# Last FFN output of a two-layer encoder on one core: sixteen of its 43 row blocks, instead of fourteen, by seven block products a pair

## The reference

```python
h = rmsnorm(x, norm_ffn[l])
gu = h @ w_ffn_in[l]
g = causal_dwconv(gu[..., :D_FF], ffn_conv_w[l], ffn_conv_b[l])
x = x + (jax.nn.silu(g) * gu[..., D_FF:]) @ w_ffn_out[l]
...
return rmsnorm(x, final_norm)
```

## Time and profile before

| What | us |
|---|---|
| median of three runs | 2070.26 |
| lowest, highest | 2069.8, 2071.41 |
| the profiled execution, its own time | 2071.34 |
| its span, first to last instruction | 2069.5 |
| PE busy | 2055.3 (99%) |
| DVE busy | 1492.8 (72%) |
| ACT busy | 1104.3 (53%) |
| last FFN output, first to last matmul | 1829.0 to 2059.1 |

### The profile page before, as it was taken

How to read it: one execution, slowest core, us unless ns; L and a number is a source line. 1 busy time by engine, 2 the same in 40 slices (tenths; PEclk the granted TensorE clock), 3 DMA queues, 4 the chain that set the end, 5 groups by cost and what they waited for, 6 DMA issues and landing times.

```text
span 2069.5 us, 32420 instructions
## 1 busy us (share of the span) xinstructions
PE 2055.3 (99%) x11522; PEld 1785.3 (86%) x11522; DVE 1492.8 (72%) x2115; ACT 1104.3 (53%) x1539; POOL 23.5 (1%) x20
## 2 busy tenths in 40 slices
PE   9999999999999999999999999999999999999998
PEld 8888888888888888888888888888888888888886
DVE  7998777676666676554489978667666767679887
ACT  6556655555555554443364656455555555555554
POOL 0001100000000000000000011000000000000000
PEclk9999999999999999999999999999999999999999
DMA  8554455655555655555565544555555565545564
GB/s 291 176 183 162 138 188 178 205 189 191 192 182 187 199 192 192 194 187 193 199 215 193 178 159 136 192 190 193 194 189 187 182 202 186 192 161 201 199 225 158
DMA packets 108370, 390.58 MB, mean 189 GB/s; under 512 B 12161, under 2 KB 12673, under 8 KB 107905
## 3 DMA queue, kind: packets, MB, share of 16 engines
q1 hardware_dynamic: 106416, 384.35, 55.6%
q10 hardware_dynamic: 1872, 5.13, 0.8%
HBM read 387.33 MB, written 2.10 MB: 188 GB/s over the span
## 4 chain that ended last, share of the span: by engine, by line
PE 97%; DVE 2%; DMA 0%; ACT 0%; issue 0%; ACTq 0%; DVEq 0%
PE bank L1414 54%; PE bank L1417 27%; PE bank L1670 3%; PE bank L1671 3%; PE bank L1672 3%; PE bank L1501 2%; PE bank L1490 1%; PE bank L1492 1%; PE bank L1491 1%; DVE wlo L1118 1%; PE bank L1554 0%; DMA par<-params 0%; PE bank L1666 0%; PE bank L1577 0%; ACT whi L675 0%
## 5 line engine op out<-in xcount | busy, mean ns | idle before, releaser
L1414 PE MATMUL bank<-xg,whi 128*128 128x512 f32 x3648 | 1136.6, 393 | 2.2 <-DVE wlo L858 2.2
L878 DVE TENSOR_TENSOR wlo<-raw,whi 128x1024 fp32r<-128x1024 f32 x642 | 780.5, 1222 | 490.1 <-ACT whi L498 489.4
L498 ACT ACTIVATE whi<-raw 128x1024 fp32r<-128x1024 f32 x642 | 673.7, 1057 | 577.2 <-PE bank L1417 559.3
L1417 PEld LDWEIGHTS bank<-xg,wlo 128*128 128x128 f32 x3648 | 685.7, 188 | 151.4
L1417 PE MATMUL bank<-xg,wlo 128*128 128x256 f32 x3648 | 720.5, 279 | 0.0
L1414 PEld LDWEIGHTS bank<-xg,whi 128*128 128x128 f32 x3648 | 553.5, 188 | 6.3 <-issue 3.3
L1414 PE MATMUL bank<-hidden,whi 128*128 128x512 f32 x688 | 213.4, 392 | 0.0
L1414 PE MATMUL bank<-mix,whi 128*128 128x512 f32 x512 | 160.7, 395 | 0.0
L1417 PEld LDWEIGHTS bank<-hidden,wlo 128*128 128x128 f32 x688 | 129.2, 188 | 28.3
L1417 PE MATMUL bank<-hidden,wlo 128*128 128x256 f32 x688 | 135.7, 279 | 0.0
L503 ACT ACTIVATE half<-bank 128x256 f32<-128x256 f32 x228 | 86.1, 382 | 63.7 <-PE bank L1417 61.2
(11 more groups left out here) (191 smaller groups left out, 1449.3 us busy)
## 6 DMA issues: line engine op xcount, KB each, us to landing
raw<-wstream SPq DMA_DIRECT2D x725, 512.0 KB, 3.3
pw_sb<-pww ACTq DMA_DIRECT2D x2, 1024.0 KB, 6.7
outT<-xt SPq DMA_DIRECT2D x8, 256.0 KB, 2.9
x<-xT SPq DMA_DIRECT2D x2, 512.0 KB, 9.8
gains<-gain_rows ACTq DMA_DIRECT2D x1, 1024.0 KB, 6.0
raw<-wstream SPq DMA_DIRECT2D x2, 256.0 KB, 4.5
x<-xT ACTq DMA_DIRECT2D x2, 256.0 KB, 5.5
x<-xT SPq DMA_DIRECT2D x2, 256.0 KB, 7.0
```

Source lines behind the costliest of these rows:

```text
L498: nc.scalar.activation(whi[:, s, slot_cols(rel)], raw[:, s, :], ACT.Copy).then_inc(hi_ready, 1)
L878: nc.vector.tensor_tensor(wlo[:, s, slot_cols(rel)], raw[:, s, :], whi[:, s, slot_cols(rel)], ALU.subtract).then_inc(lo_ready, 1)
L1414: nc.tensor.matmul(ps[bank][:], whi[:, s, blk * P:blk * P + P], mov, start=first, stop=False)
L1417: return nc.tensor.matmul(ps[bank][:, 0:S], wlo[:, s, blk * P:blk * P + P], mov[:, 0:S], start=False, stop=last)
```

## The change

There are eight pairs, (3, 4), (8, 9) and so on to (38, 39), in place of seven that began with (8, 9). So 27 ordinary pieces are left for each half, not 29. They no longer stand by three between pairs but by two or three, by a table for each half. Two of the four batches of factors move: behind slots 25 and 38 instead of 26 and 40; the fourth batch is now of two pairs. All else is unchanged, and every line behind the table is two lines further down.

```diff
-PAIRED = [(8 + 5 * i, 9 + 5 * i) for i in range(7)]
+PAIRED = [(3 + 5 * i, 4 + 5 * i) for i in range(8)]
 SINGLE = [k for k in range(FC) if not any(k in pair for pair in PAIRED)]
 LEAD = (8, 4)
+BETWEEN = ((2, 2, 3, 2, 2, 3, 2, 3), (3, 3, 3, 2, 3, 2, 3, 2))
...
     lead, rest = SINGLE[:LEAD[u]], SINGLE[LEAD[u]:]
     units = [(k,) for k in lead]
-    for i, pair in enumerate(PAIRED):
-        units += [pair] + [(k,) for k in rest[3 * i:3 * i + 3]]
-    return units + [(k,) for k in rest[3 * len(PAIRED):]]
+    for pair, n in zip(PAIRED, BETWEEN[u]):
+        units += [pair] + [(k,) for k in rest[:n]]
+        rest = rest[n:]
+    return units + [(k,) for k in rest]
...
-COMBS_AT = (5, 12, 26, 40)
+COMBS_AT = (5, 12, 25, 38)
```

## The result

The changed kernel takes 2077.59 us (median of seven executions, 2075.25 to 2078.12) against 2070.32 us for the kernel before: a ratio of 1.0033, 95% interval 1.0022 to 1.0043. That is 7.3 us slower; the forecast was 5.0 us slower, 2075.2 us, with a range of 2072.0 to 2077.6 us. The profiled execution took 2075.25 us with a span of 2073.0 us and is the shortest of the seven. Of all executions timed for this text one, of 5323 us in experiment 10, lies far outside the others; without it that experiment's median would be 2071.45 us instead of 2071.51.

What follows compares the result with a forecast made beforehand. PE, busy 99% of the span, was taken to bound the kernel, able to wait only for DVE. Terms -1.36 + 1.58 + 0.25 + 2.7 + 1.8 gave +5.0 us on 2070.26: 2075.2 us, range 2072.0 to 2077.6.

Steps and rivals of the forecast that it cites:

- the four stalls: PE idle before fe of slots 15, 28, 40 and before the last piece: about 1.8, 1.0, 2.5 and 1.7 us.
- The clock falls: Rival: half clock once or twice behind a 2.5 us stall, 1.7 us each; 2077 to 2079 us; 8%.
- Part 1: Added pair, once in each half: seven products in place of eight, six matmuls fewer, 1.36 us less on PE.
- Part 2: Gaps of two without extra work: DVE ready 1.1 us before PE is due; cost nothing, or 0.1 us.
- Part 3: Second batch, slot 12: PE arrives 2.72 us earlier at fe, DVE only 1.14; stall grows by 1.58 us.
- Part 4: Third batch, slot 25, gap of three, now behind the second piece: net +0.25 us of stall.
- Part 5: Fourth batch, slot 38, gap of two, now two pairs: PE waits for DVE before fe, +2.7 us.
- Part 6: End of second half: upper corrections delay the last piece's low half, so PE stalls, +1.8 us.
- The sum of 5.0: Whole kernel: saved products and added stalls together make it 5.0 us slower, median 2075.2 us.
- The estimate for a DVE step of 1.22 us: DVE's step between low halves: 1.22 instead of 1.14 us would add some 0.3 and 0.4 us to Part 3 and Part 4.
- The signs: Trace checks: 984 matmuls; wrong if PE waits at more places than the four stalls and the change of halves.
- The parts named for "same": Whole kernel, no measurable change: rest of forecast, fourth batch or end costing little, DVE keeping up; 0.31.

Runs made afterwards that it cites:

- experiment 10: Kernel before, seven pairs, with one ordinary piece moved from the second batch's gap to the end of the first half: 2071.51 us, ratio 1.0005.
- experiment 1: The changed kernel again, unaltered, against the kernel before: 2076.88 us against 2070.21, ratio 1.0031.
- experiment 11: As 9, with the last two single batches behind slots 30 and 42 and four pieces behind the first half's last pair: 2068.09 us, ratio 0.9989.
- experiment 8: Kernel before, seven pairs in old order, factors in smaller batches (two pairs behind slots 5 and 7, one behind 12, 26, 40): 2068.74 us, ratio 0.9992.
- 9: Against experiment 7: single batches behind d slots 11, 18, 25, 31, and three pieces instead of two behind the first half's last pair: 2067.95 us, ratio 0.9987.
- experiments 6: Changed kernel, eight pairs, pieces reordered: gaps of three where factor batches are made, seven pieces behind the second half's last pair: 2074.85 us, ratio 1.0020.
- experiment 4: Kernel before, seven pairs, three ordinary pieces moved from the second half's end to its front, four hooks three slots later: 2072.51 us, ratio 1.0011.
- Experiment 2: Changed kernel, upper corrections of the second half behind the low half of the very last piece instead of ahead of it: 2076.98 us, ratio 1.0033.
- Experiment 3: Changed kernel, fourth batch of factors behind slot 43, in a gap of three, instead of slot 38: 2074.0 us, ratio 1.0017.
- Experiment 5: Kernel before, with five extra DVE operations, results unused, behind the sums of the second half's last pair: 2075.98 us, ratio 1.0027.
- experiment 7: Piece order of experiment 6, with smaller batches of factors: two pairs behind slots 5 and 7, one behind 11, 13, 25, 38: 2071.99 us, ratio 1.0005.

## Why the prediction was right, and where it was short

The direction and the four stalls were right, and the measured 2077.59 us lies in the range. But it lies 0.01 us under the range's upper end, which is luck; the repeat in experiment 1, 6.7 us slower, is inside more clearly. The forecast itself, 2074.2 to 2076.3, was missed, and the time falls where the rival "The clock falls" had put it (2077 to 2079). The range holds it only because its upper end was drawn for one fall of the clock.

By its own parts, each against the trace of the changed kernel:

- *Part 1, fewer products:* 984 matmuls for 990, 1.36 us. Right. That it can be had shows between two traces with only small waits: the last output takes 226.9 us with eight pairs (experiment 11) and 228.2 with seven (experiment 8). In the medians 9 is 0.8 us below 8, of which 0.3 is outside the span.
- *Part 2, gaps of two without extra work cost nothing:* right, in the changed kernel and with more of them in experiments 6, 9 and 11.
- *Part 3, second batch, +1.58:* 1.55. Experiment 10 has it alone, with seven pairs.
- *Part 4, third batch, +0.25:* 0.19.
- *Part 5, fourth batch, +2.7:* 2.65 in the profiled execution. The size of the stall was right, its price was not, see below.
- *Part 6, the end, +1.8:* 1.80. The mechanism was right and experiment 4 has it alone, but the part called the low half the cause. Experiment 2 shows DVE's chain just as long behind it; the bound was both.
- *The sum of 5.0:* 4.8 in the last output of the profiled execution.
- *The time outside the span* was taken as unchanged (2076.3 for 2074.5) without a reason. It grew by 0.4 us.
- *The estimate for a DVE step of 1.22 us* (0.3 and 0.4 us more in parts 3 and 4) can hold only for the whole stalls. The growth in part 3 is one ordinary piece of PE less one step of DVE, so with 1.22 it would have been 0.1 us smaller. The step of 1.14 held: 1908.15 to 1909.29.
- *The signs:* one place more than the four and the change of halves has a wait, at 1860.89. By the letter it is a sign of being wrong; it is a wait of the kernel before that the list left out. The parts named for "same" add up to 0.33 (0.05, 0.19 and 0.09), not to the 0.31 given.
- *The rival "The clock falls", at 8%,* is the step that failed. It was dismissed with the words that here PE is full on both sides. Experiment 1 shows the clock at 0.50 for 3 us behind the stall of part 5, with PE full before and behind it, at 1.4 us (the rival had 1.7), and four of its six executions lie 1 to 2.5 us above the other two. Experiment 3, without this stall, has not this spread, and of its 3.8 us over before 3.0 are in the last output of its trace and 0.4 outside the span. Experiment 5, with such a stall in the old kernel, has the spread and the extra time. The mechanism belonged in the forecast itself: 5.0 for the stalls and, in most executions, 1.4 to 1.7 us more for what follows them. The sum would have been 6.4 to 6.7.

What stays open is what decides in a given execution whether the clock falls. Six traces have an idle time of 2.35 to 2.79 us (the change, experiments 1, 2, 5, 6 and 7), and it fell behind two of them (1 and 7). The stalls with 1.65 to 1.70 us idle were not followed by a fall in any of the five traces that have one (the change, 1, 2, 3 and 10). That the fall makes up the extra time of the executions without a trace is argued from their spread and their mean clock, not shown. Of the 6.7 us in experiment 1 nothing is left over in its trace; the 7.3 of the first comparison has a few tenths without a row.

## What to carry to other kernels

The average slack of a helping engine says little; its order says it. Lay the chain of its operations between two moments at which the leading engine depends on it beside the cover in that gap: here 1.14 us of DVE against 2.72 of PE for each ordinary piece made four stalls predictable to 0.1 us. The length of a stall is not always its whole price: look at the granted clock behind it, in more than one execution. Extra work belongs behind the operation after which the helper waits anyway, in pieces smaller than that wait and not in two short gaps that follow each other. A product saved on the leading engine pays only after that: eight pairs lost 7 us in the order of the change and won 2.4 in another, where seven pairs with the smaller batches alone won 1.7.

## What the runs showed of the hardware that I had not expected

- A stall of 2.5 us in the middle of dense matmuls can cost its length and 1.4 us more, with the granted clock at 0.50 for 3 us behind it (experiment 1), and in experiment 7 at 0.50 for at least 5.6 us behind an idle time of 2.79. The same program with the same stall need not show it: the clock stayed at 1.00 in the first trace of the change.
- Something like it happens in the first 13 us of the program. The clock was 0.50 there in four traces (before, 3, 5 and 11), in which PE had been idle for 1.8 to 2.3 us until about 8 us, and 1.00 in the nine others, idle for 0.9 to 1.6 us. The last output starts at 1828.8 to 1829.1 us in the four and at 1827.6 to 1828.4 in the nine. That is 1.0 us on average, and 1.35 between the two traces compared above, as much as six matmuls (1.36 us). So one profiled execution against another misleads by that much.
